# Two DNN blocks in sequence on one core: a Silu moved ahead of two weight splits, and one modulation tile moved behind a gating

## The reference

```python
def swiglu(h, w_gate, w_up, w_down):
    return (jax.nn.silu(h @ w_gate) * (h @ w_up)) @ w_down

# first block, layer 0, first feed-forward (called s == 0 below)
hdn = swiglu(rms_norm(x, norm_pre[l, 0]), ffn1_w_gate[l], ffn1_w_up[l], ffn1_w_down[l])
x = x + 0.5 * rms_norm(hdn, norm_post[l, 0])
...
# second block: needed only much later
mod     = (jax.nn.silu(c)     @ ada_w[layer] + ada_b[layer]).reshape(b, N_MOD, D_MODEL)
mod_ctx = (jax.nn.silu(c_ctx) @ ada_w[layer] + ada_b[layer]).reshape(1, N_MOD, D_MODEL)
```

## Time and profile before

| | |
|---|---|
| median of 3 runs (lowest, highest) | 1655.94 us (1655.23, 1656.16) |
| the profiled execution, its own time | 1655.53 us |
| its span, from the first to the last instruction | 1653.7 us |
| PE (TensorE) busy | 1644.4 us, 99% of the span |
| DVE (VectorE) busy | 1236.7 us, 75% |
| ACT (ScalarE) busy | 929.8 us, 56% |
| granted TensorE clock, mean | 1.000 of full speed |
| DMA | 361.64 MB, 219 GB/s on average |

### The profile page before, as it was taken

How to read it: one execution, slowest core, us unless ns; L and a number is a source line. 1 busy time by engine, 2 the same in 40 slices (tenths; PEclk the granted TensorE clock), 3 DMA queues, 4 the chain that set the end, 5 groups by cost and what they waited for, 6 DMA issues and landing times.

```text
span 1653.7 us, 22989 instructions
## 1 busy us (share of the span) xinstructions
PE 1644.4 (99%) x8784; PEld 1418.7 (86%) x8784; DVE 1236.7 (75%) x1639; ACT 929.8 (56%) x1401; POOL 213.6 (13%) x310
## 2 busy tenths in 40 slices
PE   9999999999999999999999999999999999999998
PEld 7888888888888888888899888888888889988887
DVE  6888776788999777778888776655756569986564
ACT  6655567655565555555467455454554558665543
POOL 1100100004311012121310011000002012310000
PEclk9999999999999999999999999999999999999999
DMA  8977553787878777787755458654667545357551
GB/s 284 345 261 258 169 191 108 239 302 247 273 250 285 272 258 241 257 312 248 249 177 187 158 174 279 195 187 142 225 221 242 197 138 199 114 180 240 187 195 64
DMA packets 102430, 361.64 MB, mean 219 GB/s; under 512 B 12720, under 2 KB 13232, under 8 KB 102320
## 3 DMA queue, kind: packets, MB, share of 16 engines
q1 hardware_dynamic: 92736, 334.73, 60.0%
q0 software_dynamic: 9440, 25.36, 4.8%
q10 hardware_dynamic: 144, 0.07, 0.0%
HBM read 355.85 MB, written 1.12 MB: 216 GB/s over the span
## 4 chain that ended last, share of the span: by engine, by line
PE 93%; DVE 3%; DMA 1%; ACT 1%; issue 1%; DVEq 0%; POOLq 0%; POOL 0%; ACTq 0%
PE dn L607 28%; PE gu L532 15%; PE tp L578 11%; PE gu L578 11%; PE tp L585 6%; PE gu L585 6%; PE dn L547 4%; PE tp L560 2%; PE gu L560 2%; DMA raw<-in_weights 1%; PE tp L565 1%; PE gu L565 1%; PE dn L578 1%; DVE w_lo L1878 1%; PE dn L532 1%
## 5 line engine op out<-in xcount | busy, mean ns | idle before, releaser
L1878 DVE TENSOR_TENSOR w_lo<-raw,w_hi 128x1024 fp32r<-128x1024 f32 x518 | 635.5, 1240 | 287.0 <-ACT w_hi L1227 283.6
L1227 ACT ACTIVATE w_hi<-raw 128x1024 fp32r<-128x1024 f32 x520 | 547.3, 1056 | 432.1 <-PE gu L585 140.3
L532 PE MATMUL gu<-w_hi,hT 128*128 128x512 f32 x832 | 259.6, 393 | 1.1 <-DVE w_lo L1871 0.5
L607 PE MATMUL dn<-w_hi,actT_hi 128*128 128x512 f32 x608 | 237.9, 391 | 0.0
L607 PE MATMUL dn<-w_lo,actT_hi 128*128 128x512 f32 x608 | 236.7, 389 | 0.0
L607 PE MATMUL dn<-w_hi,actT_lo 128*128 128x512 f32 x608 | 236.7, 389 | 0.0
L578 PE MATMUL tp<-hT,w_hi 128*128 128x512 f32 x800 | 198.9, 391 | 0.0
L578 PE MATMUL gu<-hT,w_hi 128*128 128x512 f32 x800 | 189.4, 389 | 0.0
L532 PEld LDWEIGHTS gu<-w_hi,hT 128*128 128x128 f32 x832 | 154.1, 188 | 33.9 <-DVE hT L1886 1.5
L578 PEld LDWEIGHTS gu<-hT,w_hi 128*128 128x128 f32 x800 | 150.2, 188 | 31.2
L578 PEld LDWEIGHTS tp<-hT,w_hi 128*128 128x128 f32 x800 | 147.0, 188 | 28.4
(11 more groups left out here) (368 smaller groups left out, 2111.4 us busy)
## 6 DMA issues: line engine op xcount, KB each, us to landing
raw<-in_weights SPq DMA_DIRECT2D x561, 512.0 KB, 4.3
arena<-in_ada_w SPq DMA_DIRECT2D x72, 512.0 KB, 4.4
post_row<-in_post_rows POOLq DMA_DIRECT2D x10, 512.0 KB, 5.3
pre_row<-in_pre_rows POOLq DMA_DIRECT2D x10, 512.0 KB, 7.0
mod_row<-mod POOLq DMA_DIRECT2D x9, 512.0 KB, 9.4
arena<-xn POOLq DMA_DIRECT2D x96, 32.0 KB, 4.3
shift_row<-mod POOLq DMA_DIRECT2D x5, 512.0 KB, 9.0
x<-in_x_in SPq DMA_DIRECT2D x4, 256.0 KB, 5.8
```

The lines of the kernel that those rows point to most:

```text
L532: m = pe.matmul(bank, h[:, k, t * P:(t + 1) * P], w[:, r, kk * 512:(kk + 1) * 512], start=k == 0 and q == 0, stop=k == KT - 1 and q == 2)
L607: m = pe.matmul(dn[:, t, c], a[:, k, :], w[:, r, c], start=start and q == 0, stop=stop and q == 2)
L1227: act.activation(o, i, ACT.Copy, **kw).then_inc(done, 1)
L1878: dve.tensor_tensor(w_lo[:, r, :], raw[:, n % RAW, :], w_hi[:, r, :].bitcast(F32), ALU.subtract).then_inc(lo_ready, 1)
```

## The change

Two places of the first feed-forward change. On ScalarE the Silu of the two rows c moves from behind the splits of slots 16 and 17 to ahead of them. On VectorE the first of step 2's two modulation tiles moves from behind `act_lower(1)` to behind step 2's gating. The condition is j > 2 in a branch that only the first feed-forward runs through for j == 2.

```diff
@@ act: ffn(s, n0)
                 elif not by_column(s, 0):
                     opening(s, n0, lambda step, t: gate(t, step), lambda t: half_upper(0, t))
-                if not by_column(s, 0):
-                    after_slots(n0 + 8, 2)
                 if s == 0:
                     act.wait_ge(c_loaded, 32)
                     act.activation(c_row[:, :, :], c_row[:, :, :], ACT.Silu).then_inc(c_ready, 1)
+                if not by_column(s, 0):
+                    after_slots(n0 + 8, 2)
@@ dve: ffn(s, n0), the loop over the steps
                     act_lower(j - 1)
-                    ada(j, 0)
+                    if j > 2:
+                        ada(j, 0)
                     after_slots(n, 3)
                     for t in range(TT):
                         gated(j, t, t)
+                    if j == 2:
+                        ada(j, 0)
                     ada(j, 1)
```

## The result

| | before | the change |
|---|---|---|
| median (lowest to highest), 22 runs each | 1655.98 us (1654.35 to 1657.92) | 1658.16 us (1656.90 to 1661.31) |
| ratio to before, 95% interval | | 1.0015, 1.0009 to 1.0021 |
| span of the profiled execution | 1653.7 us | 1656.5 us |
| PE busy | 1644.4 us | 1643.9 us |

The change is slower by 2.2 us between the medians (0.15% by the ratio, 1.5 to 3.5 us by its interval). TensorE's work is the same; it waits longer. In the numbering of the changed kernel the lines from 2153 on have moved by three; those named here, up to line 2085, have not, but for the Silu (1421, now 1419).

What follows compares the result with a forecast made beforehand. TensorE, busy 99% of the span, was taken to bound the kernel. Removing its old wait (-0.55 us) and adding a later one (+1.03) summed to +0.5 us on the median 1655.94: 1656.4 us, range 1655.1 to 1658.7.

Steps and rivals of the forecast that it cites:

- the likeliest case: TensorE's wait moves from step 3's head to step 4's and slightly outgrows the gain: 1656.4 us, 48%.
- one of the signs: Wrong if slot 23 lands by 61.3, TensorE waits at down product near 65.8, or a new wait after 90 us.
- half rate to the end: Rival: POOL's packets hold their share of the DMA engines until 62 us; net +2.8, 1658.7 us, 17%.
- The Silu is hidden: ScalarE: the 1.90 us Silu fits the 1.80 us idle before slot 16, but for some 0.1 us.
- The tile behind the gating takes the old wait away: VectorE gates step 2 earlier, so TensorE's 0.55 us wait at 54.89, head of step 3, goes: -0.55 us.
- SP's ada tile 4.5 us later: SP issues ada tile 2 at 54.8, not 50.28, since the first modulation tile ends later; slots 22 to 24 follow.
- net = d - 1.02: TensorE's turning at step 4: slot 23 landing d us later, less 1.02 us slack; net at least -0.55.
- d = 1.5: DMA queues: slot 23 lands 1.5 us later, at 62.3, making the new TensorE wait +1.03 us.
- middle case: DMA queues: POOL alone at 0.21 MB/us until 56, then half rates, then SP alone; slot 23 at 62.3.
- My upper end, 64.6: DMA queues: SP at half rate, 0.20 MB/us, throughout; slot 23 lands at 64.6, 3.8 us later.
- The lower end: DMA queues: POOL's loads all gone, SP at 0.41 MB/us; slot 23 lands at 60.5, 0.3 us earlier.
- the rival in which the gain stands whole: Slot 23 lands within 0.5 us of its old time, POOL's loads nearly gone: -0.55, 1655.4 us, 28%.

Runs made afterwards that it cites:

- Experiment 1: The change without its VectorE edit, so only the Silu moves: 1655.01 us, ratio to before 0.9997.
- the second profile of before: The kernel before, unedited, profiled once more: 1656.56 us in a single execution.
- experiment 3: The change with ada tile 2 loaded behind slots 22 to 24 in SP's list: 1655.10 us, ratio to before 0.9993.
- the second profile: The change, with no further edit, profiled once more: 1658.81 us in a single execution.
- experiment 4: The change with POOL's nine loads issued once TensorE has used 28 slots in place of 14: 1656.39 us, ratio to before 0.9999.
- Experiment 9: The change with POOL's nine loads issued at 16 used slots in place of 14: 1661.81 us, ratio to before 1.0033.

## Why the prediction held, and which term was off

**The direction, the place and the range held; the size was too small.** 1656.4 was forecast and 1658.16 measured, inside 1655.1 to 1658.7 and inside the 3.3 us called no change. But the loss is 2.2 us where 0.5 was forecast, outside the likeliest case's own range (1655.7 to 1657.4), and one of the signs that I had named for being wrong came: TensorE waits at the down product (66.76). A second, a new wait after 90 us (0.8 us near 421), came too, but the kernel before has it in its other profile. That the range held was in part luck: its upper end was that of the rival "half rate to the end", and no such sharing was seen. Going by the steps:

- *The Silu is hidden.* Right, but for some tenths at most: it ran at 39.95, and slots 16 and 17 at 41.75 to 44.3 without idle time between. Experiment 1 shows more than I had credited to it: it moves the chain up by 0.6 to 2.3 us, by which profiles are compared (actT_lo of step 1), and with that alone no wait is left at the head of step 3.
- *The tile behind the gating takes the old wait away, -0.55 us.* The wait went. But experiment 1 shows that the tile's move was not needed for it, and the second profile of before that it is 0 to 0.55 us, so the term was at the upper end of what the two profiles show there was to win.
- *SP's ada tile 4.5 us later with slots 22 to 24 behind it.* Right: 4.0 us (54.30), the slots right behind it, out by 56.11; experiment 3 shows that this order is the cause.
- *net = d - 1.02.* Right in form. actT_lo of step 2 came at 66.03 in place of 62.91, d = 3.1, which gives +2.1 us; 2.2 were measured between the medians, and TensorE's turning moved by 1.9 in the first pair of profiles and by 3.1 in the second. The gating ended 2.8 us later (73.56 against 70.73), so VectorE made up 0.3 on the way. The down product, which I said would matter from d = 2.2 on, waited 1.27 us, and 1.73 in the second profile.
- *d = 1.5.* **This is the step that failed, in the paragraph on how large d is.** Both rates of its middle case were wrong. POOL's queue alone does not stay at 0.21 MB/us, which was a microsecond in which only its first loads had been issued: in the change it made 0.24 to 0.40 in six of the seven from 50 to 57, and 1.86 MB in all seven. And what remained was not shared by halves, for SP's tiles got nothing for 3.7 us behind their issue and the full rate afterwards. The two errors partly cancel in the sum. They leave slot 22 at 62.61, just behind where I had put slot 23 (62.3), and slot 23 no later than 63.9. My upper end, 64.6, held it, and so the rival "half rate to the end" (1658.7) was nearer in its number, with a mechanism that the trace doesn't show. The lower end was too low as well: with POOL's loads out of the way it gave d = -0.3, and experiment 4 measured 1.1 (actT_lo at 63.97), of which 0.1 is a later issue than assumed (54.94 for 54.8). SP's queue alone moved 0.25 to 0.41 MB/us between 57 and 63 there, not 0.41 throughout. So the rival in which the gain stands whole was not to be had even without POOL.

**Round-robin against the rows.** POOL's queue was through shortly before 58, at 0.27 MB/us on average, where I had taken 0.21 from one row. The Trainium skill, "DMA: Bandwidth & Descriptors", section on queues, rings and completion order, says that each DMA engine round-robins between the queue rows that it has work for, a packet at a time; I had read from it 0.41 MB/us for POOL's queue alone and an end by 55. The trace of the change doesn't agree: behind 54.30 SP's queue had loads issued beside POOL's, and its share was nothing until 58 (0.19 MB in 58:59). Whether its packets stood before the engines by then, no run shows. What made the cost was that start: a queue issued while the other had a backlog began late. Experiment 9 shows it from the other side.

**What stays open.** Where the 3.7 us in which SP's queue moved nothing are spent was not tried. Nor is the Silu alone shown to be faster than before: 0.5 us lies within its interval.

## What to carry to other kernels

When you move an instruction that frees a buffer, look first at the queue of the engine that reloads that buffer: what it costs is not the one reload but everything that stands behind it in that queue's order. Put a load that can wait behind those that cannot, before you move compute (here, one reordering of SP's list takes back the 2.2 us). A burst of loads on one queue can delay a later issue on another by more than its share, and where the burst goes matters: here, two slots later it cost 3 us more (experiment 9), fourteen slots later it cost nothing that could be measured (experiment 4, ratio 0.9999).

## What the runs showed that was not expected

**The queue with a backlog went first.** In the change SP's queue moved nothing for 3.7 us behind its issue at 54.30, while POOL's ran; in experiment 9 POOL's queue moved nothing for 3.7 us behind 54.34, while SP's ran. Without a backlog (experiment 4) SP's queue, issued at 54.94, moved 0.04 MB in 55:56 and 0.28 in 56:57. Before, where SP's loads were issued from 50.28 while POOL's were young, SP's queue moved 0.05 MB in 52:53 and 0.25 in 53:54, and both had 0.20 to 0.21 MB/us in 59:60. VectorE's own work doesn't explain the late start in experiment 9: in the kernel before POOL's first load was issued at 49.19, beside the same reductions and splits, and its queue moved 0.17 MB in 50:51.

**A wait of 3.95 us also cost clock.** In experiment 9 the granted clock was 1.00 until 74 us, 0.50 (1.2 GHz of 2.4) in 76:78 and 0.90 in 78:80. A gate and up product of w_hi, the row of x2 at 76.87, took 1.05 us there and 0.61 at 79. The waits of 1.27 and 1.12 us in the profile of the change left no such mark: its clock is 1.00 in every stretch from 60 to 80, and so it is around the 1.73 us of the second profile (64 to 78).

**VectorE beside POOL.** The wait near 420 comes from a stretch in which POOL runs long two-input instructions. VectorE and POOL in the kernel before (timelines):

```profile
403.81 1.24 DVE L1878 TENSOR_TENSOR w_lo<-raw,w_hi 128x1024 fp32r<-128x1024 f32 x1
...
407.28 3.36 DVE L2023 CUSTOM_DVE_ANT_0 arena<-arena 128x1024 f32<-128x1024 f32 x1
...
410.57 3.41 DVE L2023 CUSTOM_DVE_ANT_0 arena<-arena 128x1024 f32<-128x1024 f32 x1
```

```profile
407.16 5.74 POOL L2672 TENSOR_TENSOR xn<-arena,pre_row 128x1024 f32<-128x1024 f32 x2
```

A split of 128 x 1024 takes 1.24 us at 403.81; the reductions of the modulation, 1.22 us at 47.88, take 3.36 and 3.41 us beside POOL's two, which taken singly last 2.40 us (to 409.56) and 3.38 us (to 412.90). The Trainium skill, "SBUF — State Buffer", section "SBUF: two separate sides", says that the port pair of the two engines is a lock and no split of the bandwidth, held for a whole instruction, and that VectorE takes part in it with two SBUF inputs against a GpSimd instruction that reads SBUF. The trace agrees: 2.2 us are added to each reduction, and each ends 1.1 us behind an end of POOL's. What TensorE waits for behind it hangs on a few tenths of a microsecond: actT_lo begins at 417.92 in this profile, with no wait, and at 418.58 in the second one of before, where TensorE was ready sooner and waited 1.22 us. That POOL's instructions are what moves this wait from one execution to the next was not tried.
